# Input first with places of its own for the first weights, and a token-major end, in a fused decoder step

## The chip, the core and the metric

The kernel runs on one core of one Trainium2 chip. The metric is the device time of one launch, in microseconds; lower is better. One launch does the whole step: the two layers, both groups of sequences, and all outputs.

## The reference, cut to what matters

A two-layer decoder trunk for a prompt group (256 tokens, one sequence) and a sample group (8 sequences of 8 tokens), 320 tokens in all, D = 1024. Each layer computes a modulation from a conditioning vector c, a mixer, and a channel mixer; layer 0 has a dense SwiGLU, layer 1 a mixture of 8 experts of which each token uses 2.

```python
mod = (silu(c) @ w_ada[l] + b_ada[l])[:, None, :]
sh1, sc1, g1, sh2, sc2, g2 = jnp.split(mod, 6, axis=-1)
h = _rmsnorm(x, norm_pre_mix[l]) * (1.0 + sc1) + sh1
mix, s_new, v_rows = _mixer(h, ...)                 # first product: h @ w_in
x = x + g1 * _rmsnorm(mix, norm_post_mix[l])
h = _rmsnorm(x, norm_pre_ffn[l]) * (1.0 + sc2) + sh2
f = _swiglu(h, ...) if l % 2 == 0 else _moe(h, ...)
x = x + g2 * _rmsnorm(f, norm_post_ffn[l])          # l = 1: the output y
# _moe: out = sum over experts of combine[..., e] * swiglu_e(h), combine = softmax of the top 2
```

All of it is fp32. The large products are made from operands split into a high part (`float32r`, one pass of TensorE) and a low part, with three products: high x high, high x low, low x high.

## The kernel before, in words

All engines run programs of their own, tied by semaphores. In front of the experts, x is kept with the channels on the partitions (X, eight tiles of 128 channels by 320 tokens).

**Weights.** Up to the experts the weights come as 512 KB units in a fixed list (UNITS, line 152). SyncE (SP) issues one DMA a unit (`load_unit`, line 454) into a ring of nine places (RAW, `RAW_UNITS`); unit n waits until unit n - 9 has been used. Units 0 to 7 are the first modulation group (scale of the first norm), 8 to 15 the second (its shift), 16 and up the first columns of w_in with other modulation groups among them. ScalarE (ACT) makes the high part of a unit (`hi_until`, line 1365), VectorE (DVE) the low part (`lo_until`, line 543).

**Start.** ACT issues the DMAs of c and then x (lines 1459 to 1463); POOL those of the constants (with the identity matrix `ident`) and of small vectors. TensorE (lines 2027 to 2069) waits for the constants, does three fillers (`warm`, line 1898: products of ones whose result nobody reads; each is one of 320 columns), turns c, multiplies units 0 and 1, waits for x and turns it in five pieces that DVE copies to X. ACT squares X, TensorE adds the squares over the partitions (`stat`), ACT takes the root, DVE the reciprocal, TensorE spreads it over the partitions (`spread_rstd`). Between these it makes the rows of the two modulation groups (`rows_unit`, line 1914, one call a unit), turns them (`turn`) and DVE adds the bias (`modulation`, line 553). From the fourth unit of group 1 on, one filler stands behind each unit. Then DVE scales x by group 0, adds the shift of group 1, and ACT and DVE make high and low operand (lines 741 to 767 and 1481 to 1490) for the first operand product, line 1939. ACT also takes an exponential for the lower bounds of the recurrence between the two copies of the rows (line 1479).

**Routing.** Behind the last norm the tokens are stored in rows (HMF, then `h_rows` in HBM, line 512), the router picks two experts a token, and for job 0 the rows of the expert's tokens are gathered by POOL (line 1840), turned by TensorE (`fill`, line 2381) and split (`gathered`, `low_fill`). While it waits TensorE does eight fillers (line 2402). The modulation group of the last gate (index 11) is made in the same stretch (`pause_turned(2)`).

**Jobs.** A job is one expert with up to 128 of its tokens: 35 pairs (512 KB twice, or 384 KB twice) of weights through a ring of seven places (MRAW); ACT makes the high part of each (`m_hi_part`), DVE the low one (`m_lo_part`), up to five pairs ahead. Eight jobs always run, as a loop; up to four extra jobs, for experts with more tokens than 128, run if needed (one does with these inputs), from a second loop whose body is skipped otherwise. At a job's last pair ACT and DVE make the result in rows of tokens (YEH, YEL), and convert the last two of the next job's first pairs. Its tokens are added to the sums SA (channels on the partitions) in the next job, by products with a placement matrix PTS (`combine`, line 2394). So that the last job can convert "next" pairs too, SP loads five pairs that nobody multiplies (line 526).

**End.** Behind the last job (line 2504 and down; DVE lines 1335 to 1355; ACT lines 1720 to 1727): the last job's tokens are added to SA tile by tile (TensorE, then DVE, then ACT's square); DVE multiplies by the gate (AM); sum of squares, root, reciprocal, spread; DVE scales SA and adds it to X; TensorE, behind 13 fillers, turns X to rows of tokens; ACT and DVE copy them; SP writes them out. POOL has always 13 gathers in its program, one behind another; those that no job has used are released by a marker that DVE sets when the last job is done (line 1337).

## Time and profile before

| | us |
|---|---|
| median of 3 runs | 2127.05 |
| lowest and highest | 2126.18 to 2130.05 |
| the profiled execution's own time | 2128.88 |
| its span, first to last instruction | 2127.0 |
| TensorE products busy in it | 2058.9 (97%) |
| VectorE busy | 1449.0 (68%) |
| ScalarE busy | 1140.9 (54%) |
| mean granted clock of TensorE | 0.987 |

The profile is of one execution. Its span is what the trace covers; 1.9 us of the execution's time lie outside. PE is the row of TensorE's products and PEld that of its weight loads, which run beside them. `<-` behind an idle time names what ended it; "issue" is time in which the engine waited for nothing that the profile shows. PEclk is the granted clock, 1.00 for 2.4 GHz and 0.50 for 1.2 GHz.

### The profile page before, as it was taken

Reading aid. Unit: us, or ns where it says so; the run is one execution under the profiler, and the core shown is the slowest. Engines: PE = TensorE matmul, PEld = TensorE weight load, DVE = VectorE, ACT = ScalarE, POOL = GpSimd, SP = SyncE. Lnnn points to the kernel's source line nnn. Section 1 sums busy time; section 2 is a strip of 40 time slices with the busy share of each in tenths; the row PEclk is TensorE's granted clock in tenths of the full one; section 3 lists DMA queues with packets and bytes.
Section 4 is the critical chain, followed back from the end, with each engine's and each line's share of the span. In section 5 each row is a group of like instructions: output and inputs, shape, how many; then the busy total and the mean of one; then the engine's idle time right before and its main releaser. Section 6 shows DMA issues by size and latency. Waiting matters only on the chain. (4 is left out here: it accounts for less than half of the span.)

```text
span 2127.0 us, 34921 instructions
## 1 busy us (share of the span) xinstructions
PE 2058.9 (97%) x13483; PEld 1843.5 (87%) x13483; DVE 1449.0 (68%) x1610; ACT 1140.9 (54%) x1149; POOL 131.9 (6%) x170
## 2 busy tenths in 40 slices
PE   7999999999999999999999899999999999999997
PEld 4999999888999899989999688888888888888885
DVE  4476545555444456745454689898989898898986
ACT  3434334344333343432443568686777777686764
POOL 2200003200000030000230100000000000000000
PEclk9999999999999999999999899999999999999998
DMA  9635465564666454435654599999999999999994
GB/s 314 214 109 164 129 197 172 194 192 132 216 198 222 125 180 128 125 106 171 188 171 159 201 329 393 327 398 334 372 361 353 374 327 400 327 400 330 391 343 179
DMA packets 244643, 528.79 MB, mean 249 GB/s; under 512 B 18199, under 2 KB 142217, under 8 KB 244530
## 3 DMA queue, kind: packets, MB, share of 16 engines
q1 hardware_dynamic: 234512, 496.56, 66.5%
q0 software_dynamic: 9648, 29.29, 4.4%
q8 instruction: 81, 1.33, 0.3%
q10 hardware_dynamic: 370, 1.35, 0.2%
q14 instruction: 32, 0.26, 0.0%
HBM read 514.54 MB, written 12.59 MB: 248 GB/s over the span
## 5 line engine op out<-in xcount | busy, mean ns | idle before, releaser
L1665 ACT ACTIVATE mhi<-mraw 128x2048 fp32r<-128x2048 f32 (+1 forms) x320 | 579.3, 1821 | 216.1 <-DMA mraw<-in_w_exp_up 89.7
L1135 DVE TENSOR_TENSOR mlo<-mraw,mhi 128x2048 fp32r<-128x2048 f32 (+1 forms) x319 | 681.2, 2164 | 10.3 <-ACT mhi L1665 9.7
L549 DVE TENSOR_TENSOR wlo<-raw,whi 128x1024 fp32r<-128x1024 f32 x244 | 289.1, 1212 | 313.6 <-ACT whi L1373 312.7
L1939 PE MATMUL ps<-h1h,whi 128*128 128x320 f32 x1248 | 386.1, 322 | 7.2 <-DVE h1l L656 3.9
L1940 PE MATMUL ps<-h1l,whi 128*128 128x320 f32 x1248 | 371.6, 310 | 0.0
L2426 PE MATMUL ps<-mhi,xeh 128*128 128x512 f32 (+1 forms) x864 | 327.4, 379 | 2.1 <-DVE xel L1154 1.7
L2427 PE MATMUL ps<-mhi,xel 128*128 128x512 f32 (+1 forms) x864 | 322.0, 373 | 0.0
L1373 ACT ACTIVATE whi<-raw 128x1024 fp32r<-128x1024 f32 x244 | 247.8, 1046 | 119.2 <-PE ps L2325 44.8
L1939 PEld LDWEIGHTS ps<-h1h,whi 128*128 128x128 f32 x1248 | 236.2, 189 | 23.7 <-issue 18.0
L1940 PEld LDWEIGHTS ps<-h1l,whi 128*128 128x128 f32 x1248 | 236.3, 189 | 0.0
L2432 PE MATMUL ps<-mlo,xeh 128*128 128x512 f32 (+1 forms) x864 | 225.0, 372 | 0.0
L1985 PE MATMUL ps<-h1h,wlo 128*128 128x320 f32 x1248 | 209.3, 310 | 0.0
L1985 PEld LDWEIGHTS ps<-h1h,wlo 128*128 128x128 f32 x1248 | 189.0, 188 | 0.4 <-issue 0.4
L2426 PEld LDWEIGHTS ps<-mhi,xeh 128*128 128x128 f32 x864 | 162.7, 188 | 23.3 <-issue 2.0
L2427 PEld LDWEIGHTS ps<-mhi,xel 128*128 128x128 f32 x864 | 162.9, 189 | 19.8
L2432 PEld LDWEIGHTS ps<-mlo,xeh 128*128 128x128 f32 x864 | 159.7, 188 | 22.9
L2463 PE MATMUL ps<-mhi,gth 128*128 128x512 f32 x396 | 157.8, 399 | 0.0
L2464 PE MATMUL ps<-mhi,gtl 128*128 128x512 f32 x396 | 154.7, 391 | 0.0
L2469 PE MATMUL ps<-mlo,gth 128*128 128x512 f32 x396 | 106.3, 390 | 0.1
L2469 PEld LDWEIGHTS ps<-mlo,gth 128*128 128x128 f32 x396 | 74.3, 188 | 16.3 <-DVE mlo L1135 0.5
L2464 PEld LDWEIGHTS ps<-mhi,gtl 128*128 128x128 f32 x396 | 74.5, 188 | 14.3
L2463 PEld LDWEIGHTS ps<-mhi,gth 128*128 128x128 f32 x396 | 74.4, 188 | 14.4
(394 smaller groups left out, 2686.9 us busy)
## 6 DMA issues: line engine op xcount, KB each, us to landing
mraw<-in_w_exp_down SPq DMA_DIRECT2D x198, 512.0 KB, 8.3
mraw<-in_w_exp_gate SPq DMA_DIRECT2D x154, 512.0 KB, 5.3
mraw<-in_w_exp_up SPq DMA_DIRECT2D x144, 512.0 KB, 6.5
raw<-in_w_in SPq DMA_DIRECT2D x128, 512.0 KB, 3.9
raw<-in_w_ada SPq DMA_DIRECT2D x72, 512.0 KB, 3.7
mraw<-in_w_exp_gate SPq DMA_DIRECT2D x72, 384.0 KB, 3.6
mraw<-in_w_exp_up SPq DMA_DIRECT2D x72, 384.0 KB, 4.6
pause<-in_w_ada SPq DMA_DIRECT2D x24, 512.0 KB, 6.5
```

The source lines that it names most:

```text
L549: V.tensor_tensor(WLO[:, u % RAW_UNITS, 0:w], RAW[:, u % RAW_UNITS, 0:w], WHI[:, h % HI_UNITS, 0:w].bitcast(F32), ALU.subtract).then_inc(l ...
L1135: V.tensor_tensor(MLO[:, n % RAW_RING, 0:w], MRAW[:, n % RAW_RING, 0:w], MHI[:, n % HI_RING, 0:w].bitcast(F32), ALU.subtract).then_inc(m_l ...
L1373: A.activation(WHI[:, h % HI_UNITS, 0:w], RAW[:, u % RAW_UNITS, 0:w], ACT.Copy).then_inc(hi_made, 1)
L1665: A.activation(MHI[:, n % HI_RING, 0:w], MRAW[:, n % RAW_RING, 0:w], ACT.Copy).then_inc(m_hi, 1)
L1939: M.matmul(out_, w, v[0], start=start, stop=False, skip_group_check=True)
L1940: M.matmul(out_, w, v[1], start=False, stop=False, skip_group_check=True)
L1985: ins = M.matmul(PS[:, 2 * j + m, 0:T], w[1][:, s], parts[0][:, k * T:(k + 1) * T], start=False, stop=(k == KD - 1), skip_group_check=True)
L2426: M.matmul(o_, XEH[:, k, :], hi_[:, s], start=(k == 0), stop=False)
L2427: M.matmul(o_, XEL[:, k, :], hi_[:, s], start=False, stop=False)
L2432: ins = M.matmul(PS[:, GROUP_BANKS[g][2 * i + j], 0:w], XEH[:, k, :], lo_[:, s], start=False, stop=(k == KD - 1))
L2463: M.matmul(PS[:, DOWN_BANKS[h], :], GTH[:, kf, :], hi_[:, s], start=(kf == 0), stop=False)
L2464: M.matmul(PS[:, DOWN_BANKS[h], :], GTL[:, kf, :], hi_[:, s], start=False, stop=False)
```

## The change

**Start.** x is loaded by SP, in front of all weights, no longer by ACT. Units 0 to 7 get places of their own (in memory that the operands take later), each with a semaphore of its own; the ring of nine places begins with unit 8, so the first unit that waits for a place is unit 17. TensorE's first three fillers become six products of 128 columns of ones that don't wait for the constants; units 0 and 1 are multiplied behind the turning of x; the five fillers among the rows of group 1 go, and three stay behind its turning instead of four. ACT loads the root's table before it squares (a small root of ones), and the exponential for the lower bounds comes behind the operand pieces.

**Routing.** The gate of the last step is computed here (`gate_dve(1, 48, G2)`), and TensorE makes from it GT: the gate in token-major form, 128 partitions by 1024 channels for the prompt (all rows alike) and 64 by 1024 for the samples. That takes 16 fp32 products with the identity and four copies by ACT. It sits between the pick and the gathered rows, with three fillers behind it instead of eight. DVE first waits until the stored rows are in HBM, since the new tables lie where they came from.

**Jobs.** The conversions of pairs 3 and 4 (ACT) and 2 and 3 (DVE) of a job are made at its head instead of at the end of the job before. Three pairs that nobody multiplies are loaded instead of five.

**End.** TensorE turns the old sums SA straight into the accumulators (six tiles: three groups of tokens by two halves of the channels; `is_transpose`), and adds the last job's tokens with two products of 512 columns a tile. ACT squares each tile with a sum along it (`accum_out`), DVE multiplies it by GT; the root and reciprocal of a [128, 3] table follow. TensorE turns X into banks that have come free, and DVE adds the scaled tile to it. SP writes each 128 tokens as they are ready.

```diff
+GT_BANKS = ((2, 3), (5, 1))
+Z_BANKS = ((0, 1), (4, 5), (6, 7))
+XT_BANKS = ((2, 3), (0, 1), (4, 5))
+LAST_TILES = [(t, h) for t in range(3) for h in range(2)]
+        def raw_count(u):
+            return 16 * (u // RAW_UNITS + (u % RAW_UNITS >= KD))
# SP
-                if n >= RAW_UNITS:
+                if n < KD:
+                    sp.dma_start(PAUSE[1][n][:, :].unsqueeze(1), src).then_inc(first_in[n], 16)
+                    return
+                if n >= KD + RAW_UNITS:
                     sp.wait_ge(unit_used, n - RAW_UNITS + 1)
+            sp.dma_start(XTM[:, 0:2, :], a["x_prompt"][0].rearrange("(t p) d -> p t d", p=P)).then_inc(xtm, 16)
+            sp.dma_start(XTM[0:TS, 2, :], a["x_sample"].rearrange("s t d -> (s t) d")).then_inc(xtm, 16)
             for n in range(len(UNITS)):
...
-            for n in range(HI_RING):
+            for n in range(HI_RING - 2):
...
+            for t in range(2):
+                sp.wait_ge(sem("y_out"), 2 * t + 2)
+                sp.dma_start(out["yp"][0, P * t:P * t + P, :], XTM[:, t, :]).then_inc(sem("y_stored"), 16)
# DVE, routing
+            pause_turned(2)
+            gate_dve(1, 48, G2)
+            dve.wait_ge(hd_stored, 16 * TT)
+            V.tensor_copy(GE[:, :, :].rearrange("p k (s t) -> p k s t", s=NS), seq(AM)).then_inc(sem("ge_made"), 1)
             m_lo_part(0, 0)
             m_lo_part(0, 1)
-            pause_turned(2)
...
             def job_dve(job, first=False):
+                m_lo_part(job, 2)
+                m_lo_part(job, 3)
                 for p in range(PAIRS):
...
-                        m_lo_part(job, p + HI_RING - 2)
-                    if p != PAIRS - 2:
+                    if p < PAIRS - 2:
                         m_lo_part(job, p + HI_RING - 1)
# DVE, end
+            see.step(V.memset(ZS[:, :, :], 0.0), sem("zs_zero"))
+            dve.wait_ge(sem("gt_out"), 4)
+            for i, (t, h) in enumerate(LAST_TILES):
+                n, g = (P, 0) if t < 2 else (TS, 1)
+                dve.wait_ge(sem("z_squared"), i + 1)
+                V.tensor_tensor(XTM[0:n, t, 512 * h:512 * h + 512], PS[0:n, Z_BANKS[t][h], :],
+                                GT[0:n, g, 512 * h:512 * h + 512], ALU.mult).then_inc(sem("z_gated"), 1)
+            see.step(V.tensor_tensor(ZT[:, :], ZS[:, 0, :], ZS[:, 1, :], ALU.add), sem("z_summed"))
+            see.next(sem("z_root"))
+            st(V.reciprocal(ZT[:, :], ZT[:, :]))
+            for t, h in LAST_TILES:
+                see.next(sem("xt_in"))
+                V.scalar_tensor_tensor(XTM[0:n, t, 512 * h:512 * h + 512], XTM[0:n, t, 512 * h:512 * h + 512],
+                                       ZT[0:n, t:t + 1], PS[0:n, XT_BANKS[t][h], :], ALU.mult, ALU.add)\
+                    .then_inc(sem("y_out"), 1)
# ACT, start, routing and end
+            A.activation(ROOT1[:, :], ONES[:, 0:1], ACT.Sqrt)
             act.wait_ge(aux_out, 6)
...
+            act.wait_ge(hd_stored, 16 * TT)
+            act.wait_ge(sem("gt_in"), 1)
+            for g in range(2):
+                for h in range(2):
+                    n = (P, TS)[g]
+                    A.activation(GT[0:n, g, 512 * h:512 * h + 512], PS[0:n, GT_BANKS[g][h], :], ACT.Copy)\
+                        .then_inc(sem("gt_out"), 1)
             for k in range(2):
                 gathered(k, k)
...
+            A.activation(ROOT1[:, :], ONES[:, 0:1], ACT.Sqrt)
+            see.next(sem("zs_zero"))
+            for i, (t, h) in enumerate(LAST_TILES):
+                n = P if t < 2 else TS
+                act.wait_ge(sem("z_in"), i + 1)
+                A.activation(ZQ[0:n, i, :], PS[0:n, Z_BANKS[t][h], :], ACT.Square, accum_out=ZS[0:n, h, t:t + 1])\
+                    .then_inc(sem("z_squared"), 1)
+            see.next(sem("z_summed"))
+            A.activation(ZT[:, :], ZT[:, :], ACT.Sqrt, bias=EPST[:, 0:1], scale=1.0 / D).then_inc(sem("z_root"), 1)
# TensorE, routing and end
-            warm(8, 3)
+            pe.wait_ge(sem("gate_made"), 4)
+            pe.wait_ge(sem("ge_made"), 1)
+            pe.wait_ge(sem("hm0_out"), TT)
+            for g in range(2):
+                for d in range(KD):
+                    gate = GE[:, d, :] if g else AM[:, d, 0:1].broadcast_to([P, P])
+                    ins = M.matmul(PS[0:(P, TS)[g], GT_BANKS[g][d // 4], d % 4 * P:(d % 4 + 1) * P], gate, ident,
+                                   start=True, stop=True, skip_group_check=True)
+            ins.then_inc(sem("gt_in"), 1)
+            warm(3, 4)
...
-            warm(4, 7)
+            pe.wait_ge(m_aux_out, extra * JAUX + (NE * JAUX + AHEAD))
+            for t, h in LAST_TILES:
+                for d in range(4):
+                    M.matmul(PS[0:n, Z_BANKS[t][h], d * P:(d + 1) * P], SA[:, 4 * h + d, t0:t0 + n], ident,
+                             start=(d == 0), stop=False, is_transpose=True, skip_group_check=True)
             pe.wait_ge(y_made, extra + (NE + 1))
+            for t, h in LAST_TILES:
+                M.matmul(PS[0:n, Z_BANKS[t][h], :], PTS[:, t0:t0 + n], YEH[:, s], start=False, stop=False,
+                         skip_group_check=True)
+                M.matmul(PS[0:n, Z_BANKS[t][h], :], PTS[:, t0:t0 + n], YEL[:, s], start=False, stop=True,
+                         skip_group_check=True).then_inc(sem("z_in"), 1)
+            for i, (t, h) in enumerate(LAST_TILES):
+                if t:
+                    pe.wait_ge(sem("z_gated"), i - 1)
+                for d in range(4):
+                    ins = M.transpose(PS[0:n, XT_BANKS[t][h], d * P:(d + 1) * P], X[:, 4 * h + d, t0:t0 + n], ident)
+                ins.then_inc(sem("xt_in"), 1)
```

## Rows read from the trace of the kernel before

**Rows 1.** By stage: window, length; busy PE, PEld, DVE, ACT, POOL; clock, DMA share, GB/s.

```profile
0.00:41.30 41.30, 28.71 (x262) 14.80 (x262) 11.72 (x32) 11.47 (x21) 5.56 (x19) 0.96 0.88 308
41.30:52.10 10.80, 7.75 (x48) 6.97 (x48) 8.84 (x22) 6.52 (x13) 5.45 (x9) 1.00 0.96 334
52.10:1211.50 1159.40, 1121.13 (x8755) 1050.19 (x8753) 618.31 (x898) 466.74 (x627) 108.28 (x131) 0.99 0.54 168
1211.50:2089.60 878.10, 877.53 (x4276) 754.66 (x4277) 789.02 (x626) 644.70 (x474) 9.82 (x9) 1.00 0.96 358
2089.60:2127.00 37.40, 23.74 (x147) 16.91 (x145) 21.10 (x35) 11.49 (x17) 2.83 (x3) 0.76 0.25 83
```

**Rows 2.** Chain that ended last, behind the last job: start, length (us), what.

```profile
2092.82 0.08 DVEq L1332
...
2095.29 0.80 issue
```

**Rows 3.** By stage again, the start cut finer for the DMA.

```profile
0.00:15.00 15.00, 5.66 (x26) 3.21 (x30) 0.45 (x3) 2.34 (x2) 4.99 (x18) 1.00 0.88 291
15.00:25.00 10.00, 8.43 (x122) 4.92 (x114) 4.02 (x9) 3.71 (x9) 0.00 (x0) 1.00 1.02 397
25.00:30.00 5.00, 3.35 (x28) 1.99 (x32) 0.65 (x1) 0.89 (x2) 0.00 (x0) 0.73 0.36 145
```

**Rows 4.** Order of time, the start: start, length, engine, line, operation, count, wait.

```profile
9.01 3.57 PE L1901 MATMUL ps<-cf,ones 128*128 128x320 f32 x6 [9.01 <-DMA cf<-in_const_f]
...
15.89 1.64 PE L2045 MATMUL ps<-cf,xtm 128*128 128x128 f32 x8
...
20.78 2.99 ACT L1393 ACTIVATE t<-x 128x320 f32<-128x320 f32 x8 [14.64 <-DVE x L730]
...
24.28 1.28 ACT L1405 ACT_TABLE_LOAD   x1 [0.52 <-PE ps L1868]
...
28.01 3.22 PE L1910 MATMUL ps<-raw,csf 128*9 128x256 f32 x32
...
33.86 3.22 DVE L751 SCALAR_TENSOR_TENSOR ht<-x,am,ps 128x256 f32<-128x256 f32 x8
...
37.64 0.62 PE L1910 MATMUL ps<-raw,csf 128*9 128x256 f32 x8
```

**Rows 5.** Busy time in a stretch of the start.

```profile
28.00:30.00 2.00, 2.00 (x21) 0.77 (x24) 0.00 (x0) 0.00 (x0) 0.00 (x0) 0.50 0.03 12
```

**Rows 6.** Order of time, the routing and the start of job 0.

```profile
1203.37 2.25 POOL L1840 DMA_INDIRECT xg<-h_rows,idx  x1 [21.31 <-DVE idx L1149]
...
1209.51 1.08 ACT L1670 ACTIVATE xeh<-ps 128x512 fp32r<-128x512 f32 x2 [6.04 <-PE ps L2385]
...
1211.56 0.67 PE L2426 MATMUL ps<-mhi,xeh 128*128 128x512 f32 x1 [1.65 <-DVE xel L1154]
```

**Rows 7.** Groups by line: one fp32 product of 128 columns is two records.

```profile
L2235 PE MATMUL ps<-im,ktm 128*128 128x128 f32 x256 | 33.4, 274 | 0.0
```

**Rows 8.** Order of time, the head of an expert job.

```profile
1411.14 6.68 DVE L1135 TENSOR_TENSOR mlo<-mraw,mhi 128x2048 fp32r<-128x2048 f32 x3
...
1416.14 1.07 PE L2432 MATMUL ps<-mlo,xeh 128*128 128x512 f32 x4
```

**Rows 9.** Order of time, the end.

```profile
2089.64 1.26 ACT L1698 ACTIVATE yeh<-ps,sw 128x512 fp32r<-128x512 f32 x2 [0.87 <-PE ps L2469]
2090.36 1.41 DVE L1288 SCALAR_TENSOR_TENSOR yel<-ps,sw,yeh 128x512 fp32r<-128x512 f32 x2 [1.10 <-ACT yeh L1698]
...
2101.64 0.95 POOL L1840 DMA_INDIRECT xg<-h_rows,idx  x1 [3.71 <-DMA xg<-h_rows,idx]
...
2108.41 9.40 PE L1901 MATMUL ps<-cf,ones 128*128 128x320 f32 x26
...
2117.65 2.78 PE L2518 MATMUL ps<-cf,x 128*128 128x128 f32 x24
...
2119.59 1.88 DVE L1355 COPY xtm<-ps 128x512 f32<-128x512 f32 x3 [4.98 <-PE ps L2518]
```

More of the change, by code:

```diff
@@ L398, in build @@
         raw_in = [sem(f"raw_in{n}") for n in range(RAW_UNITS)]
+        first_in = [sem(f"first_in{n}") for n in range(KD)]
         hi_made, lo_made = sem("hi_made"), sem("lo_made")
@@ L1477, in _ @@
             rows_copy(0)
-            see.next(sem("lb_shifted"))
-            A.activation(LT[:, 0:2, :], LT[:, 0:2, :], ACT.Exp).then_inc(sem("lb_exp"), 1)
             rows_copy(1)
@@ L1490, in _ @@
                                  bias=MOD[:, mod_tile(0, SH1) + d, 0:1]).then_inc(sem("h_hi"), 1)
+            see.next(sem("lb_shifted"))
+            A.activation(LT[:, 0:2, :], LT[:, 0:2, :], ACT.Exp).then_inc(sem("lb_exp"), 1)
             hi_until(HI_UNITS)
@@ L2054, in _ @@
             M.transpose(PS[:, b, P:P + 82], VR[0:82, 1, :], CF[0:82, C_ID:C_ID + 82]).then_inc(aux_in, 1)
-            for k in range(2, 5):
+            for k in range(2):
                 rows_unit(k, k, 2)
@@ L2058, in _ @@
                 stat(k == 0, k == KD - 1)
+            rows_unit(2, 2, 2)
+            rows_unit(3, 3, 2)
             spread_rstd(4)
-            for k in range(5, KD):
+            for k in range(4, KD):
                 rows_unit(k, k, 2)
```

82 lines of the change are left out of this document (26 added, 56 removed).

## Prediction

> **What bounds the kernel now.** I read the busy time by stage first [rows 1]. TensorE is busy 877.5 of the 878.1 us of the nine expert jobs (eight, and one of the extra ones) and 1121 of the 1159 us of the layers ahead of them: these stages run at TensorE's pace, and a change that only shifts them shifts the end by as much. Two stretches are not at its pace: the first 41.3 us, where TensorE has 28.7 us of work, fillers among them, and the last 37.4 us with 23.7 us, again fillers among them, at a granted clock of 0.76. The change works in both, and a little at the routing. So I read next the chain of waits behind the last job [rows 2], the DMA by stage [rows 3], and the order of time at the start [rows 4], at the routing, at a job's head and at the end.
>
> **The start.** The first product waits for the shift of modulation group 1, whose last weights (unit 15) are multiplied at 37.64 us [rows 4]; the product follows at 41.3, where the second stage of rows 1 begins, 3.7 us later. What holds unit 15 back is a stall: with nine places, units 9 and up wait for units that TensorE uses only after it has turned x, and x lands at 15.89. DMA moves 291 GB/s up to 15 us, 397 up to 25 and then 145 up to 30 [rows 3]. With eight places more, all of units 0 to 16 are issued with no wait. Bytes: x 1.31 MB, constants and conditioning 0.40, sixteen units of 0.524: 10.1 MB. By 25 us 291 x 15 + 397 x 10 = 8.3 MB have moved in any case; the other 1.8 MB take 4.5 us at 397: unit 15 is in at 29.5 us, unit 7 (5.9 MB) at 18.9, unit 16 (first of w_in) at 30.8. The product then comes at 29.5 + 3.7 = 33.2, 8.1 us earlier.
>
> Does the other input arrive in time? x is first in SP's queue: with the constants 1.7 MB, at 291 GB/s 6 us, in by 7. The constants, which TensorE's first product waits for until 9.01, decide, and behind them the turning of c. The turning of x starts near 11 instead of 15.89, at the low clock, and takes 5 us instead of the 4.9 from 15.89 to the squares at 20.78: squares from 16. The squares and their sums take 3.5 us as before (20.78 to 24.28), the root's table load of 1.28 us is out of the chain, and root, reciprocal and spread take 2.45 (from its end at 25.56 to 28.01): 22 us. Then five row products; the row at 28.01 has four of them in 3.22 us at half clock: 4.0, so 26. From there to the end of the scaled x is 5.8 us (31.23 to 37.08) [rows 4]: 32 us, when DVE could have had the shift at 31.2. So this branch, not DMA, ends last by 0.8 us if the clock stays low, and 1.5 us ahead if it is high. I take 7.2 us for the start. Bounds: 9, with the clock high throughout, and 4, if the constants or x land 3 us later than I think and the clock stays low through the first products.
>
> The Exp for the lower bounds is moved behind the operand pieces on ACT: its table load and itself, 1.5 us, come inside the 10.8 us of the first operand products, in which ACT has 6.5 us of work [rows 1]; nothing, at most 0.3.
>
> The five fillers between the row products go, and TensorE then waits for weights, with 0.6 us of work (the row at 37.64) to 0.8 (at 28.01) in the 1.3 us that a unit of 0.524 MB takes at 397 GB/s [rows 3, 4]. In this trace it was at the low of its two levels (1.2 instead of 2.4 GHz) after a pause: the stretch at 28 us has a granted clock of 0.50 [rows 5]. The three fillers left, six records like the six of 3.57 us at 9.01 [rows 4], reach from 31.5 to 35 at that clock: up to 1.8 us behind the operands. The products that follow wait for DVE twice anyway (7.75 us of work in 10.8 [rows 1]), which swallows most of it. The Trainium skill's page "TensorE: Matmul & The Clock Gate" (Part 1, the HAM clock gate) speaks against this edit: the low clock is the default and only recent activity lifts it. The trace agrees; by it the rival "cold start" below gets its chance.
>
> On the table load the Trainium skill ("ScalarE: Activation LUTs", What ACT_TABLE_LOAD costs) counts 1.28 us and as much again for a drain, 2.66 in all. The row has 1.28 us and the root right behind it [rows 4]; by the page's figure ACT's squares at the end would begin 1.4 us later and that branch would end at 2108.4, a fifth of a microsecond behind the sum below. The measured duration decides.
>
> **The routing.** Gate tables are now made here, under the gather. Before, ACT gets the gathered rows, turned, at 1209.51, and job 0 begins at 1211.56 [rows 6]. New work on TensorE: from 1203.9 (DVE's index is out before the gather's start at 1203.37, say at 1202.5, and it has then the modulation, the gate and a copy of 512, by size 0.3 + 0.2 + 0.7 us) 16 fp32 products of 128 columns, two records each of 0.13 us [rows 7]: 4.3 us, then three fillers instead of eight, 1.6: 1209.8. On ACT four copies of 512 (0.54 each, as the two of 1.08 in rows 6) from 1208.3 hold the high halves of the gathered rows until 1210.6, where they began at 1209.51: 1.1 us late, and so is job 0. The wait of DVE for the stored rows costs nothing, as the gather waits for the same. Low side: -0.6, if the clock, low in the first 3 us of job 0 before, stays high. High side: +5.4, if the sixteen products run at half clock. I take +1.1. The two low parts on DVE move from before to after the job's start in the same order: nothing.
>
> **Job boundaries.** Two conversions each on ACT and DVE pass from the end of a job to the head of the next, same order. What changes is that the loop's jump has no conversion queued in front of it. In the chain behind the last job DVE's queue spends 2092.82 to 2095.29, 2.5 us, on the three extra jobs not taken [rows 2], 0.8 a jump at most. The conversion at 1411.14 is the first of three and its product is read at 1416.14 [rows 8]: over 2 us to spare. Nothing.
>
> **The end.** Before: last product to end of span, 37.4 us. After: the high half of the last sums comes as before at 2089.64, DVE's low half ends at 2091.77 [rows 9]. TensorE meanwhile turns the old sums: 24 transposes, 2.8 us as the 24 at 2117.65, to 2092.4; then 12 products of 512 columns at 0.23 [rows 8], the first pair at 2092.9, the last at 2095.2. ACT: its sequencer too has 2.5 us of jumps behind 2090.3, then the root's table load and a small root, 1.5: 2094.3 is the first square, not 2092.9. Six squares of 512 with a sum: 0.63 each from the two at 2089.64 (1.26), 0.7 with the sum, whose cost no row shows (bounds 0.54 and 1.0): 2098.5. DVE's product follows each (0.7): 2099.2; sum, root, reciprocal 0.8: 2100.0; six combined operations of 0.71 (two in 1.41 at 2090.36): 2104.3. The output: before, 5.5 us from the last copy (2121.47) to the end, with 1.31 MB; now only 0.26 MB follow the last operation, at 0.8 for issue, 1.0 and 0.9: 2107.
>
> Beside it runs POOL's chain: the gathers left over, three where one extra job is used, start when DVE sets the marker and are 4.6 us apart (2096.98, 2101.64 and so on, [rows 9]), 14.6 us from marker to last landing. The marker comes at 2093.6 (the second low half is issued when the first ends, near 2091.05, and 2.5 us of jumps follow), so this ends at 2108.2. It was hidden; it now ends last, by about a microsecond. The end: 2127.0 - 2108.2 = 18.8 us gained. What is gone: two conversions on ACT and DVE (4.5 us, 2091.68 to 2096.16), sums handed back and forth one by one with their squares, and 13 fillers of 9.4 us, behind which the last transposes began only at 2117.65. Bounds: 20, if the jumps are cheaper; 14, if squares take 1.0 and TensorE's and ACT's jumps add 2 us more.
>
> **Sum.** -7.2 + 1.1 - 18.8 = -24.9. Against the profiled execution (span 2127.0, its own time 2128.9) this is a span of 2102.1; the median of the runs, 2127.05, lies 1.8 below the profiled one's time, and 2127.05 - 24.9 = 2102. What this kernel's measurement can tell from no change is 0.2%, 4.3 us.
>
> **Rivals.**
> - Cold start (0.13): x and constants later, low clock through the first products, the start gives 3 us or less: 2107. For it: fillers gone, and 0.50 in rows 5; against it: DVE's pace hides much.
> - Gate tables at half clock or ACT's copies worse than thought (0.10): +4.3 at the routing: 2106.5. For it: TensorE now waits for DVE just before, where it had fillers.
> - The end is bound by ACT, squares at 1.0 and longer jumps (0.09): 2106.
> - The uncovered jump (0.03): a jump at a job's end, now in front of DVE's and ACT's next conversions, has 2 us to spare; what it costs over that stops TensorE at each of eight boundaries. From 5.1 us a jump on (8 x 3.1 = 25) the gain is used up; at 5.7 it is 8 x 3.7 = 29.6, a kernel slower than before, 2131.6. Against it: 0.8 us is the longest piece in rows 2.
> - The end hardly gains (0.03): 2120 and more, if the output is held by something that the rows don't show.
>
> The forecast has 0.62, its own range 2097 to 2105.5; the range over the first three rivals is 2097 to 2110. Faster 0.95, same 0.02, slower 0.03.
>
> **What would show it.** Right: DMA near 397 GB/s without a gap from 15 to 30 us; the first operand product near 34; job 0 about 6 us earlier than 1211.56; TensorE still over 99% busy in the jobs; some 19 us from the last expert product to the end, with a gather last. Wrong: a first product behind 38, a gap in front of job 0 of over 4 us more, idle TensorE at a job's head, or an end stretch over 24 us.

## The result, and where the time went

The first comparison gave 2114.1 us against 2128.6 (medians of four runs each), a ratio of 0.9941 with an interval of 0.9922 to 0.9960; a second, with six runs of the changed kernel and sixteen of the one before, gave 2110.9 against 2128.7, ratio 0.9932 (0.9915 to 0.9949). The medians differ by 14.4 and 17.8 us, and both intervals lie below 1. I had forecast a gain of 24.9 us (2102.0), with a range that ended at 2110: the direction was right, the gain 7 to 10.5 us too large.

The stages of the changed kernel's trace, in the columns of [rows 1] (window, length; busy PE, PEld, DVE, ACT, POOL; clock, DMA share, GB/s), and behind them the start cut finer as in [rows 3]:

```profile
0.00:34.30 34.30, 23.26 (x257) 13.81 (x257) 11.95 (x32) 10.23 (x20) 5.55 (x19) 1.00 0.97 355
34.30:45.30 11.00, 7.82 (x48) 7.05 (x49) 8.36 (x20) 6.55 (x14) 5.03 (x8) 1.00 1.07 371
45.30:1204.20 1158.90, 1118.71 (x8776) 1049.82 (x8775) 619.65 (x902) 470.29 (x632) 107.27 (x132) 0.99 0.54 169
1204.20:2085.00 880.80, 877.90 (x4278) 753.05 (x4279) 790.06 (x626) 654.85 (x483) 9.82 (x9) 1.00 0.95 354
2085.00:2107.70 22.70, 8.05 (x60) 6.80 (x58) 9.53 (x18) 6.56 (x17) 2.83 (x3) 0.75 0.39 127
...
0.00:15.00 15.00, 8.79 (x46) 7.49 (x46) 3.59 (x8) 3.83 (x4) 4.98 (x18) 1.00 0.87 308
15.00:25.00 10.00, 9.31 (x164) 4.46 (x162) 2.69 (x10) 3.70 (x10) 0.00 (x0) 1.00 1.02 408
25.00:30.00 5.00, 2.48 (x32) 0.47 (x32) 4.15 (x10) 0.00 (x0) 0.00 (x0) 1.00 1.04 391
```

The start is as forecast: 391 GB/s where 145 stood, and the second stage begins at 34.3 instead of 41.3. The end fell from 37.4 to 22.7 us, not to 18.6. And the stage that I had charged with nothing, the nine jobs, grew from 878.1 to 880.8 us; TensorE is idle 2.9 us in it where it was idle 0.6, and ScalarE has 10 us more of work. The layers' 1158.9 us hide a gain and a loss (the router is reached sooner, the routing is longer). All the pieces, from one trace of each kernel that was run (the experiments below name them):

```
us             first    to the   to the  pick to  nine    end      span   mean
               product  router   pick    job 0    jobs    stretch         clock
before          41.35   1143.6   16.27   10.39    878.1   37.4    2127.0  0.987
after           34.30   1141.2   16.64   12.10    880.8   22.7    2107.7  0.992
after_again     35.22   1138.4   19.18   12.21    881.0   22.5    2108.5  0.989
start_only      35.28   1140.8   18.49   10.39    876.1   37.4    2118.5  0.988
rest_only       40.05   1140.8   14.43   13.32    881.4   22.5    2112.4  0.991
jobs_only       41.91   1144.3   16.43   10.40    882.6   32.2    2127.9  0.987
silu_first      34.29   1142.6   19.26   12.12    877.5   22.5    2108.3  0.989
sums_first      34.16   1145.8   18.15   12.09    876.7   22.5    2109.4  0.987
gathers10       35.40   1144.9   18.57   11.87    881.2   16.7    2108.6  0.987
routing         34.38   1142.1   14.42   11.51    881.1   22.5    2106.1  0.990
combo_dyn       34.59   1139.5   18.19   10.43    877.7   16.6    2097.0  0.992
combo_sums      34.48   1137.3   16.63   10.44    876.4   16.6    2091.9  0.994
combo_nofill    34.97   1144.0   14.43   11.50    875.7   16.6    2097.2  0.988
combo_zs        34.46   1146.2   16.42   10.46    875.7   15.8    2099.1  0.990
```

The columns are: the first operand product; from it to the router's first product; from there to the pick; to job 0's first product; to the high half of the last sums (yeh); to the end. They add up to the span. Two of them, the layers and the way to the pick, spread over 9 and 5 us between these traces, without order by kernel, and by 2.8 and 2.5 us between the two traces of the changed kernel itself; stretches at half clock fall in other places each time. The whole time follows the clock loosely: among the runs of the kernel before that stand beside the experiments the run with the highest mean clock, 0.993, took 2116.7 us and the one with the lowest, 0.981, took 2136.4. The other four columns repeat within about 0.6 us where the code is the same and no half-clock stretch lies in them, and the reading below goes by these. The profiled execution of the changed kernel is the fastest of its first four, with the highest mean clock (0.992 against 0.986 to 0.988); where the others lost their time no trace shows.

**The start** of the changed kernel, in order of time (start, length, engine, line, operation, count, wait):

```profile
9.93 3.95 PE L2078 MATMUL ps<-cf,xtm 128*128 128x128 f32 x16 [0.33 <-DVE csf L742]
...
20.99 1.92 PE L1940 MATMUL ps<-pause,csf 128*9 128x256 f32 x32
...
27.88 0.62 PE L1940 MATMUL ps<-raw,csf 128*9 128x256 f32 x8 [0.66 <-DMA raw<-in_w_ada]
...
30.53 0.62 PE L1940 MATMUL ps<-raw,csf 128*9 128x256 f32 x8 [0.74 <-DMA raw<-in_w_ada]
...
31.92 1.78 PE L1931 MATMUL ps<-cf,ones 128*128 128x320 f32 x6
34.30 0.39 PE L1973 MATMUL ps<-h1h,whi 128*128 128x320 f32 x1 [0.59 <-DVE h1l L786]
```

x is turned from 9.93, before the 11 that I took; the row products run at the high clock (32 records in 1.92 us, 3.22 in [rows 4]); unit 15 is multiplied at 30.53 and the product follows 3.8 us later. The last five rows of group 1 each wait for their DMA and come 1.28 to 1.36 us apart: the start is now at the pace of the DMA. The other branch, the scaled x, ends at 29.2 (VectorE, 3.22 us from 26.00).

**The routing.** The gate tables between the pick and job 0:

```profile
1194.35 3.14 PE L2441 MATMUL ps<-cf,am 128*128 128x128 f32 x16 [1.42 <-DVE am L702]
1197.42 2.44 PE L2441 MATMUL ps<-cf,ge 128*64 128x128 f32 x16
1199.79 1.88 PE L1931 MATMUL ps<-cf,ones 128*128 128x320 f32 x6
...
1199.96 2.04 ACT L1709 ACTIVATE gt<-ps 128x512 f32<-128x512 f32 x4 [5.56 <-PE ps L2441]
1202.15 1.09 ACT L1693 ACTIVATE xeh<-ps 128x512 fp32r<-128x512 f32 x2
...
1204.20 0.49 PE L2469 MATMUL ps<-mhi,xeh 128*128 128x512 f32 x1 [1.66 <-DVE xel L1176]
```

The sixteen products take 5.5 us, not 4.3, for part of them run at half clock (granted clock 0.62 over the first half of them, 0.78 over the second). ScalarE's gathered rows (xeh) come behind its four copies, which end at 1202.0, and behind their own turning, which TensorE begins at 1201.51 when its three fillers are done; xeh starts at 1202.15. It makes 12.1 us from pick to job 0 against 10.39.

**A job's head.** The boundary behind the second of the nine jobs, in order of time on each engine: the changed kernel (ScalarE, then VectorE, then TensorE's weight load), and the same place in start_only, where the conversions are still at the end of the job before.

```profile
1399.69 1.27 ACT L1728 ACTIVATE yeh<-ps,sw 128x512 fp32r<-128x512 f32 x2 [1.70 <-PE ps L2512]
1400.98 1.28 ACT L1688 ACT_TABLE_LOAD   x1
1402.27 3.72 ACT L1688 ACTIVATE mhi<-mraw 128x2048 fp32r<-128x2048 f32 x2
1406.01 1.28 ACT L1717 ACT_TABLE_LOAD   x1
...
1409.35 4.49 DVE L1157 TENSOR_TENSOR mlo<-mraw,mhi 128x2048 fp32r<-128x2048 f32 x2 [0.57 <-ACT mhi L1688]
1413.76 0.48 DVE L1329 TENSOR_TENSOR sa<-sa,ps 128x320 f32<-128x320 f32 x1
...
1414.29 0.19 PEld L2430 LDWEIGHTS ps<-pts,yeh 128*128 128x128 f32 x1 [0.85 <-DVE sa L1329]
```

```profile
1400.59 1.27 ACT L1708 ACTIVATE yeh<-ps,sw 128x512 fp32r<-128x512 f32 x2 [0.63 <-PE ps L2482]
1401.74 3.72 ACT L1675 ACTIVATE mhi<-mraw 128x2048 fp32r<-128x2048 f32 x2
1405.48 1.28 ACT L1697 ACT_TABLE_LOAD   x1
...
1413.70 0.48 DVE L1316 TENSOR_TENSOR sa<-sa,ps 128x320 f32<-128x320 f32 x1
...
1414.38 0.19 PEld L2410 LDWEIGHTS ps<-pts,yeh 128*128 128x128 f32 x1
```

In start_only the first sum (sa) ends 13.6 us behind yeh, and TensorE's third combine product, which needs it, loads its weights at 13.8: 0.2 us to spare. In the changed kernel there are two table loads. One stands in front of the first two conversions, which start 1.43 us later; the other stands behind them, where start_only has its only one, and holds the conversions that follow. VectorE makes the low parts behind ScalarE's high parts, so it loses 0.4 us to the first load and waits 0.57 us for the third high part, behind the second load. The sum stands behind these low parts in VectorE's queue and starts at 14.1 instead of 13.1, and TensorE waits. The waits of weight loads for that sum over the nine jobs (us, times, longest):

```profile
PEld ps L2430 <- DVE sa L1329: 6.2, 8, 0.9
```

The Trainium skill ("ScalarE activation tables: per-element evaluation and per-set limits", Table sets in the compiler and the runtime) says that the back end places table loads per block, the greedy longest run first. A load of its own at the head of the loop's body is in keeping with "per block"; that it takes one set for the two copies and another from the Silu on is not the longest run, since the copies behind the Silu need no load. The rows decide: two loads at job 0's head and at each of the seven boundaries behind it. Only the head of the extra job, which has a loop of its own, shows none; in start_only it has none either.

**The end**, ScalarE, VectorE, SP, POOL, and the time from issue to landing:

```profile
2084.97 1.27 ACT L1728 ACTIVATE yeh<-ps,sw 128x512 fp32r<-128x512 f32 x2 [0.30 <-PE ps L2512]
...
2089.06 0.60 ACT L1754 ACTIVATE zq<-ps 128x512 f32<-128x512 f32 x1 [0.69 <-DVE zs L1363]
2089.56 0.19 ACT L1754 ACTIVATION_READ_ACCUMULATOR zq<-ps 128x1 f32 x1
...
2088.85 0.15 DVE L1361 COPY spare<-sw 128x1 f32<-128x1 f32 x1 [1.75 <-issue]
...
2094.26 4.03 DVE L1377 SCALAR_TENSOR_TENSOR xtm<-xtm,zt,ps 128x512 f32<-128x512 f32 x6
...
2098.32 0.52 SPq L554 DMA_DIRECT2D out_ys<-xtm  x1
...
2089.75 0.94 POOL L1870 DMA_INDIRECT xg<-h_rows,idx  x1 [46.78 <-DVE spare L1361]
2094.36 0.94 POOL L1870 DMA_INDIRECT xg<-h_rows,idx  x1 [3.67 <-DMA xg<-h_rows,idx]
2099.74 0.94 POOL L1870 DMA_INDIRECT xg<-h_rows,idx  x1 [4.43 <-DMA xg<-h_rows,idx]
...
out_yp<-xtm SPq DMA_DIRECT2D x2, 512.0 KB, 4.8
out_ys<-xtm SPq DMA_DIRECT2D x1, 256.0 KB, 4.3
xg<-h_rows,idx POOLq DMA_INDIRECT x3, 5.1
```

VectorE's last operation ends at 2098.3, 13.3 us behind yeh (forecast 14.7), and the last of the output lands at 2098.3 + 4.3 = 2102.6. A gather ends last, as forecast: the third lands 5.3 us after 2099.74, at 2105.0. But the second and third are 5.4 us apart, not 4.6 as the first and second, and the span goes on for 2.7 us behind the last landing.

### The profile page after: what moved, and what is told of

Read it like the earlier page. It is cut to its first block and busy times, and to the rows that moved or that the text cites. A ratio compares the mean times of both kernels' runs of the same rounds, so it can differ in the third digit from the quotient of the medians.

```text
span 2107.7 us, 34719 instructions
## 1 busy us (share of the span) xinstructions
PE 2035.7 (97%) x13413; PEld 1830.5 (87%) x13413; DVE 1439.6 (68%) x1595; ACT 1148.5 (54%) x1162; POOL 130.5 (6%) x170
## 5 line engine op out<-in xcount | busy, mean ns | idle before, releaser
L1157 DVE TENSOR_TENSOR mlo<-mraw,mhi 128x2048 fp32r<-128x2048 f32 (+1 forms) x317 | 677.1, 2163 | 15.7 <-ACT mhi L1688 14.8
L2475 PEld LDWEIGHTS ps<-mlo,xeh 128*128 128x128 f32 x864 | 159.4, 188 | 22.7
L2512 PEld LDWEIGHTS ps<-mlo,gth 128*128 128x128 f32 x396 | 74.3, 188 | 15.8
L2506 PEld LDWEIGHTS ps<-mhi,gth 128*128 128x128 f32 x396 | 74.4, 188 | 14.4
```

Source lines behind the costliest of these rows:

```text
L1157: V.tensor_tensor(MLO[:, n % RAW_RING, 0:w], MRAW[:, n % RAW_RING, 0:w], MHI[:, n % HI_RING, 0:w].bitcast(F32), ALU.subtract).then_inc(m_l ...
L2475: ins = M.matmul(PS[:, GROUP_BANKS[g][2 * i + j], 0:w], XEH[:, k, :], lo_[:, s], start=False, stop=(k == KD - 1))
L2506: M.matmul(PS[:, DOWN_BANKS[h], :], GTH[:, kf, :], hi_[:, s], start=(kf == 0), stop=False)
L2512: ins = M.matmul(PS[:, DOWN_BANKS[h], :], GTH[:, kf, :], lo_[:, s], start=False, stop=(kf == KF - 1))
```

## The experiments

**after_again**, the changed kernel unchanged.

> The changed kernel once more, unchanged. Its first four runs lay between 2109.5 and 2117.3 us (8 us apart), with the profiled one the fastest, while the kernel before lay within 4 us. Theory (clock): the spread comes from stretches of low granted clock that fall in other places from run to run, so the mean clock of a run and its span go together (0.992 with 2107.7, 0.986 with 2112 to 2115.5 so far), and the middle of five more runs is 2112 to 2115. Rival (fixed loss): there is no such tie, and the five runs lie within 2 us of each other. Ratio to the kernel before expected at 0.993 to 0.994.

Six runs of 2110.3 to 2116.0 us, median 2110.9; the two longest, 2116.0 and 2114.2, are those with the lowest mean clock (0.986, 0.987; the others have 0.988 and 0.989). The tie to the clock holds in this set, and the median is 1.1 us under the expected range.

**start_only**, the kernel before with the start of the change alone.

> The kernel before with the start of the change alone (x first on SyncE, places of their own for the first modulation group, no fillers among the rows, the exponential moved). Theory (it acts as the traces of the two kernels show it): first operand product near 34.3 us instead of 41.35, and all of it reaches the end: 7 us under the kernel before, ratio 0.9967. Rival (clock): with fillers gone the clock is low in more or other places of the first layers, and 1 to 4 us of the 7 are given back in most runs: 3 to 6 us, ratio 0.9972 to 0.9986.

Median of eleven runs 2121.0, ratio 0.9966 (0.9952 to 0.9980): 7.2 us. The first product came at 35.3, not 34.3: its trace is at half clock (0.50) from 30 to 36 us, and those of after_again and gathers10 are too. From the first product to the router the eleven traces with the new start have 1137.3 to 1146.2 us, on average 1142.1, and the three with the old one (before, jobs_only, rest_only) 1140.8 to 1144.3, on average 1142.9: nothing shows that clock is given back later, though the spread of 9 us could hide a few microseconds. The interval of the ratio, 4.3 to 10.2 us, also allows the rival's upper end.

**rest_only**, the changed kernel with the start of the one before.

> The changed kernel with the start of the kernel before (ScalarE loads x behind c, no places of their own for units 0 to 7, fillers among the rows). First operand product at 41.3 to 41.4 us, nine jobs 880.8 to 881.3 us, end 22.5 to 22.8 us: 9 to 10 us under the kernel before, 7 over the changed kernel. Rival (the parts are not independent): the jobs or the end stretch differ by over 1 us from the changed kernel's.

One run, 2114.2 us: jobs 881.4 and end 22.5, as in the changed kernel; the parts are independent there. The first product came at 40.05, over a microsecond earlier than in the two other traces with that start (41.35 and 41.91), and pick to job 0 took 13.3 us, since all sixteen products of the gate tables fell in a stretch of low clock (3.75 and 3.05 us for the two halves, granted clock 0.56 over them).

**jobs_only**, the kernel before with the job part alone:

```diff
             def job_act(job):
+                m_hi_part(job, 3)
+                m_hi_part(job, 4)
                 A.activation(SPARE[:, 0:1], ONES[:, 0:1], ACT.Silu)
...
-                        m_hi_part(job, p + HI_RING - 1)
-                    if p != PAIRS - 2:
+                    if p < PAIRS - 2:
```

> The kernel before with the job part of the change alone (two conversions on ScalarE and VectorE passed from a job's end to the next one's head, three spare pairs loaded instead of five). Theory (table load): the extra table load of 1.28 us is there at each of the eight looped jobs' heads, and the nine jobs take 880.5 to 881.3 us instead of 876.1 to 878.1. Rival (the longer jobs come from the new routing, tables or end): they stay at 876 to 878. In the end stretch the part alone takes away the conversions of 4.4 us behind the last product: 37.4 falls to 33 to 34 us.

Jobs 882.6 us and end 32.2 (expected 33 to 34): the end wins 5.2 us and the jobs lose 4.5 by the two traces. The one run took 2129.7 us, against a median of 2126.2 for the kernel before, whose runs go from 2116.7 to 2133.6. The wait is there, in a kernel with the old start, routing and end:

```profile
PEld ps L2395 <- DVE sa L1304: 5.7, 7, 0.9
```

The job time is 1.3 us over the range expected. The head of job 0 lies in a half-clock stretch (0.50 from 1213.1 to 1216.1), as it does in the kernel before, whose line is this:

```profile
1211.60:1215.00 3.40, 3.40 (x8) 2.67 (x9) 3.40 (x2) 3.38 (x3) 0.00 (x0) 0.52 0.00 0
```

Half of such a stretch is lost by TensorE, 1.6 of these 3.4 us (an estimate from the clock of 0.52). It accounts for most of the 2.0 us by which the kernel before, with 878.1, is longer than start_only, with the same jobs and 876.1. So the change's price in the jobs is 880.8 to 881.4 less 876.1, 4.7 to 5.3 us, of which the two profiled executions set side by side show only 2.7.

**silu_first**, one line moved:

```diff
             def job_act(job):
+                A.activation(SPARE[:, 0:1], ONES[:, 0:1], ACT.Silu)
                 m_hi_part(job, 3)
                 m_hi_part(job, 4)
-                A.activation(SPARE[:, 0:1], ONES[:, 0:1], ACT.Silu)
```

> One line moved: at a job's head ScalarE's small Silu of ones comes in front of the two conversions that the change put there, not behind them. Theory (table load): the conversion in front of the Silu needs a table of its own at the head of the loop's body, 1.28 us more on ScalarE in every job, and that is what makes the nine jobs 880.7 us long instead of 878.0. Without it the jobs are back at 878.0 to 878.3, the wait of TensorE for VectorE's sum in the combine step (2.8 us in all) goes, and the time is 2.5 us under the changed kernel's. Rival (uncovered jump): the loop's jump with no conversion queued in front of it is what costs; then the jobs stay at 880.7 and the time stays within 0.5 us.

One table load a job is left, the nine jobs take 877.5 us, and the time is 2110.5 (2105.7 to 2111.8), a ratio of 0.9917 (0.9899 to 0.9935) where the changed kernel has 0.9932. The expected 2.5 us are not seen in the times (0.4 by the medians), whose intervals overlap; the 3.3 to 3.9 us are seen in the job column. The same boundary as above:

```profile
1405.22 1.28 ACT L1715 ACT_TABLE_LOAD   x1
...
1406.62 9.12 ACT L1688 ACTIVATE mhi<-mraw 128x2048 fp32r<-128x2048 f32 x5
...
1417.44 0.48 DVE L1329 TENSOR_TENSOR sa<-sa,ps 128x320 f32<-128x320 f32 x1
```

The load that is left is again in front of the first two conversions, which start 2.69 us behind yeh (1403.93), no earlier than the changed kernel's 2.58. What is gone is the load behind them, and with it VectorE's wait for the third high part: the sum starts 13.5 us behind yeh instead of 14.1. In start_only it was 13.1. So the wait is not gone:

```profile
PEld ps L2430 <- DVE sa L1329: 2.3, 7, 0.6
```

**sums_first**, both table loads left as they are, VectorE's order changed:

```diff
+                    summed = [u for u in SIDE[p] if u[1] == "combine"]
+                    for s, _, k in summed:
+                        dve.wait_ge(m_aux_in, job * JAUX + (s + 1))
+                        V.tensor_tensor(SA[:, k, :], SA[:, k, :], PS[:, 4 + s % 2, 0:T], ALU.add)\
+                            .then_inc(m_aux_out, 1)
                     if p < PAIRS - 2:
                         m_lo_part(job, p + HI_RING - 1)
```

> The changed kernel with one thing in another order on VectorE: in the pairs 2 to 9 of a job, the sum of the last job's tokens (sa) comes in front of the pair's conversion, not behind it; the extra table load stays. Theory (queue behind the conversions): TensorE's third combine product of a job waits for VectorE's first sum, which stands behind the conversions that now start 1.4 us later; with the sum in front of one conversion of 2.28 us it is in time in spite of the table load. The wait of weight loads for sa (6.2 us in 8 times) goes and the nine jobs fall from 880.8-881.4 to 876 to 877 us. Rival (ScalarE's later high parts hold TensorE itself, or the jobs are longer for another reason, code or records): they stay over 880.

The same lines are taken out where they stood, behind the conversion. Both table loads are there and the jobs take 876.7 us; no wait for the sum is left, only this, of a kind that the kernel before has too (0.5 us, once):

```profile
PEld ps L2515 <- DVE mlo L1157: 0.9, 2, 0.7
```

The time from one job's yeh to the next one's, in the traces above, shows how the loss is made up (differences of the starts of yeh in order of time; the last one ends with the extra job):

```
us                      job 0 to 1   next six, each   to the extra job's
before, start_only      98.0         97.22            97.22
changed kernel          97.9         97.91 to 97.94   97.70
silu_first              98.0         97.35 to 97.37   97.68
sums_first              98.0         97.22            97.23
```

At each of the six boundaries the changed kernel loses 0.7 us: 0.57 by the second load (silu_first takes it away) and 0.14 by the moved conversions with one load in front of them. With the sum ahead of a conversion both cost nothing. The last boundary has no table load and still loses 0.48, in silu_first too. There VectorE passes from its first loop to the second, over a jump, a wait and the reading of the number of extra jobs, and no longer has a conversion queued in front of that. The changed kernel:

```profile
1990.02 6.70 DVE L1157 TENSOR_TENSOR mlo<-mraw,mhi 128x2048 fp32r<-128x2048 f32 x3 [0.61 <-issue]
...
2001.63 0.19 PEld L2430 LDWEIGHTS ps<-pts,yeh 128*128 128x128 f32 x1 [0.61 <-DVE sa L1329]
```

That fits the uncovered jump of my rivals, with 0.2 us to spare instead of 2; no run takes it away by itself. With the sum ahead of a conversion (sums_first) it costs nothing either. So the loss in all its parts comes from the sum that stands behind the moved conversions with 0.2 us to spare; the table loads and, once, this jump use that up.

**gathers10**, POOL's program without the three gathers whose rows no job reads:

```diff
-            for job in range(NE + EXTRA + 1):
+            for job in range(NE + 2):
...
-            pool.wait_ge(xg_in, 16 * (NE + EXTRA + 1))
+            pool.wait_ge(xg_in, 16 * (NE + 2))
```

> The changed kernel with 10 gathers in POOL's program instead of 13: the three whose rows no job reads (with these inputs, where one extra job is used) are left out. Theory (the left-over gathers end last): the last output write lands about 4.7 us ahead of the end of the span with them, and the writes themselves get a little faster since no gather runs beside them; the end stretch falls from 22.8 to 18 us and the time by 4.5 to 5 us. Rival 1 (something behind the output, common to both): the 2.66 us between the last gather's landing and the end of the span stay as they are behind the output's landing; then the gain is 2 us. Rival 2: the writes of the output hold the end in any case, gain under 1 us.

The end is 16.7 us, 5.9 less, more than any of the theories gave; median 2107.2 against the changed kernel's 2110.9, ratio to the kernel before 0.9904 (0.9887 to 0.9920). The last writes:

```profile
2105.30 0.52 SPq L554 DMA_DIRECT2D out_ys<-xtm  x1
...
out_yp<-xtm SPq DMA_DIRECT2D x2, 512.0 KB, 2.6
out_ys<-xtm SPq DMA_DIRECT2D x1, 256.0 KB, 2.9
```

With no gather beside them the writes land after 2.6 and 2.9 us instead of 4.8 and 4.3, and the span ends 0.4 us behind the landing at 2108.2 (span 2108.6). The 2.7 us behind the last gather are tied to a gather being last: six traces with 13 gathers have 2.6 to 2.7 there, and the five without the left-over ones have 0.4 behind the last write. What happens in them no record shows. The Trainium skill ("DMA: Bandwidth & Descriptors", Queues, rings and completion order) says that each DMA engine takes turns, packet by packet, between the queues it has work for; by that writes and gathers slow each other down, and the landings agree.

**routing**, the gathered rows in front of the copies, no fillers there, the table's second half in other banks:

```diff
-GT_BANKS = ((2, 3), (5, 1))
+GT_BANKS = ((2, 3), (5, 4))
...
             for n in range(3):
                 m_hi_part(0, n)
+            for k in range(2):
+                gathered(k, k)
             act.wait_ge(hd_stored, 16 * TT)
...
-            for k in range(2):
-                gathered(k, k)
...
-            warm(3, 4)
```

> The changed kernel with the routing alone mended as in combo_dyn. Theory (the four copies of the gate table and the three fillers stand in front of the gathered rows): pick to the first product of job 0 falls from 12.2 us (with a low clock there; 12.1 in the first profile of the changed kernel) to 10.4 to 10.7, what it is without the gate tables (10.39). Rival (TensorE's 16 products themselves are what is late, 5.6 us at the low clock from 1195.1): they end at the same place, the rows are turned behind them, and only the copies' 2 us less 0.1 or nothing is won: 11.5 and more.

TensorE's wait for the four copies, in front of job 0, goes as well; VectorE waits for them instead, in front of its clearing of SW. One run, 2107.9 us. Pick to job 0 took 11.5 us, as the rival has it. Here all sixteen products ran at a low clock (0.57 granted over them), 3.75 and 2.90 us, as they did in combo_nofill, which has the same routing and also shows 11.5; in the three other kernels below that have it they took 5.5 us together and it is 10.4. Both have a part: copies and fillers in front of the rows cost 1.7 us (12.1 to 10.4), the products a further 1.1 when the clock is low for all of them.

**combo_dyn**, three mends at once; POOL's gathers for extra jobs under a condition each:

```diff
+            for k in range(EXTRA):
+                with pool.If(extra > k):
+                    pool.wait_ge(idx_made, NE + 2 + k)
+                    pool.indirect_dma_start(XG[:, :], None, HD, bass.IndirectOffsetOnAxis(IDX[:, 0:1], 0)).then_inc(xg_in, 16)
+                    pool.wait_ge(xg_in, 16 * (NE + 2 + k))
```

> The changed kernel with three mends: the small Silu in front of the two conversions at a job's head (as in silu_first); POOL issues a gather behind the ninth only for extra jobs that are used, under a condition for each (general, unlike gathers10); and at the routing ScalarE takes the gathered rows in front of the four copies of the gate table, TensorE's three fillers there go, and the sample half of the table lies in banks 5 and 4, which job 0 needs only behind its first sum. By the parts: jobs -3.3 (877.5 instead of 880.9 us), end -5.9 (16.7 instead of 22.6), routing -1.5 (pick to job 0 10.7 instead of 12.2 us): 10.7 us under the changed kernel's 2111 to 2113, so 2100 to 2102, ratio to the kernel before 0.987. Rival: the parts overlap or the conditions on POOL cost as much as a gather saves; 2104 or more.

Median 2099.8 against 2126.2 for the kernel before, ratio 0.9888 (0.9868 to 0.9909). Jobs 877.7, end 16.6, pick to job 0 10.4: each within 0.3 us of what was expected, and the conditions on POOL cost nothing that shows.

**combo_sums**, combo_dyn with VectorE's order of sums_first.

> combo_dyn and sums_first together: the 2.3 us of waits for sa that were left in combo_dyn go, nine jobs 876.1 to 876.6 instead of 877.7 us, end stretch 16.6, and the time is 1.3 us under combo_dyn's (2099.8 against a kernel before of 2126.2): ratio 0.988. Rival: conversions that now start half a microsecond later are late in their turn, jobs 877.5 or more.

Jobs 876.4. The time, 2101.4 in four runs (2093.7 to 2102.9, ratio 0.9884, 0.9868 to 0.9901), isn't under combo_dyn's and can't tell 1.3 us.

**combo_nofill**, combo_sums without the three fillers at the start.

> combo_sums without the three fillers behind the turning of group 1. In four of eight traces with the changed start the first operand product came at 35.2 to 35.4 us with the fillers at half clock in front of it, in the others at 34.3 to 34.6. Theory (fillers only hold the product back): it comes at 34.2 to 34.4, 0 to 1 us earlier, and the first 60 us are no longer otherwise; time 0 to 1 us under combo_sums. Rival (they hold the clock up): the first operand products run at half clock from 34 us on, and what they gain is lost before 60 us: time the same or up to 2 us over.

The product came at 34.97, no earlier (it waited 2.1 us for VectorE's operand), and the clock in 30 to 40 us was 0.52 instead of 0.83 in combo_sums. The time is 2100.0, ratio 0.9877 (0.9861 to 0.9894). Nothing is won or lost that the times can tell. The rival's low clock was there in the one trace, and the stretch before 60 us was not shorter: ScalarE's table load at 47.7 us comes at 47.2 to 47.4 in the other three.

**combo_zs**, combo_sums with the clearing of the table for the sums of squares ahead of the extra jobs' loop.

> combo_sums with VectorE's clearing of the table for the sums of squares moved from behind the extra jobs' loop to in front of it. In the trace of combo_sums ScalarE is ready for the first square at 2078.66 us and waits until 2079.36 for that clearing, which stands behind VectorE's jumps of 1.76 us over the extra jobs not taken. Theory (those jumps now stand in the chain of the output): the first square comes 0.6 to 0.7 us earlier behind the last expert product, the end stretch is 15.9 to 16.1 instead of 16.6 us; in the time this is less than can be measured, 2098.5 to 2101 at a kernel before of 2126 to 2128. Rival (the squares wait for TensorE's tiles): the stretch stays at 16.5 or more.

End 15.8 us, and the first square 3.3 us behind yeh instead of 4.1. The time, 2100.4 (2097.1 to 2101.7), ratio 0.9880 (0.9859 to 0.9901), is the same as that of the three before it within what can be told. These four kernels are 24 to 26 us faster than the kernel before by their ratios, and some 9 to 12 us faster than the changed kernel.

## Why the prediction was wrong, step by step

- The start, -7.2 (bounds 4 to 9): 7.05 in the profiled pair and 7.2 by start_only. The mechanism was right: DMA without a gap, unit 15 last, the table load out of the chain. That the figure fits so well is in part luck: unit 15 was used at 30.5, a microsecond behind the 29.5 of the sum, and the scaled x, taken to end last at 32 with a low clock, ended at 29.2 with a high one. The first product comes at 34.2 to 34.6, or at 35.2 to 35.4 in the three traces at half clock from 30 us on; in combo_nofill, at half clock but without fillers, at 34.97, so of that the fillers have some 0.3 us, not "up to 1.8".
- The rival "cold start" came in part, as that low clock in three of the ten traces with the fillers, at a price of about 1 us for the first product; a gain of "3 us or less" it did not make.
- The routing, +1.1: +1.5 to +1.8 in five traces with the new routing and the new start, +2.9 in rest_only. The mechanism was right; the sixteen products were sized for the high clock, 4.3 us, and take 5.3 to 5.5, and 6.7 in rest_only. The rival "gate tables at half clock" is partly true each time, at 0.4 to 0.7 us over the sum's 1.1 and at 1.8 in rest_only, not at 4.3 (and 2102 + 4.3 is 2106.3, not the 2106.5 that it says).
- **The step that failed is "Job boundaries. ... same order ... Nothing."** It costs 4.7 to 5.3 us. The order on ScalarE is the same, conversions and then the small Silu; but the boundary of the loop's body now lies in front of the conversions, and there they get a table load of their own. And the slack that I read, "over 2 us to spare" [rows 8], was that of the conversion's own reader. The operation queued behind the conversions on VectorE, the first sum, had 0.2 us. With the sum in front of a conversion (sums_first) the jobs are back at 876.7, loads and all. I asked what waits for the moved instruction, not what waits for those behind it.
- I took the 878.1 us of [rows 1] as the jobs' undisturbed length. Up to 2.0 of it was a half-clock stretch at job 0's head; I had named it, at 0.6.
- The end, -18.8 (bounds 14 to 20): -14.7. That POOL's chain ends last was right. It was mis-sized by 4.1 us, the second term that failed. I read gathers 4.6 us apart from a time with no other traffic [rows 9]; beside the output the last two are 5.4 apart and the last one lands after 5.3, so that marker to last landing is 16.2 us and not 14.6. And the 2.7 us from the last landing to the end of the span were put at nothing. The branch I worked out in more detail, ScalarE's and VectorE's, was right within 1.4 us (squares 0.57 apart, not 0.7), and without the gathers that branch ends at 16.7 us. On the root's table the measured 1.28 us held: its root follows right behind, as in [rows 4], with no drain as long again.
- The sum with what was measured: -6.7 for the start (41.35 less 34.7, the mean of the ten first products with the fillers), +1.7, +4.9, -14.7: -14.8, where the runs have -14.4 and, by the second ratio, -14.5. That is closer than the traces warrant: with the mean of the three old first products, 41.1, the start is -6.4, and the two noisy columns are left out.

The range, 2097 to 2110, was built from the rivals' prices; the largest loss was none of them. "The uncovered jump" looked at the right place and came true at one boundary, for 0.5 us, but it was weighed against 2 us of slack where the queue had 0.2.

## What to carry to other kernels

When an instruction is moved, look for the least slack among all that stand behind it in its engine's queue, not for its own reader's; a sum with 0.2 us to spare turned two table loads at a job's head into a loss of 0.7 us a job. Where copies stand at the head of a loop's body and another function behind them, look in the trace for a load in front of each; here the Silu in front of the copies saved one of the two. Work that nobody reads is free only while something else ends last: count the left-over transfers again when the end becomes shorter, with the traffic that will then run beside them.

## What the runs showed of the hardware that I had not expected

- Copies at the head of a loop's body load a table of their own, and the Silu behind them another: 1.28 us each, eight times. The head of the extra job, in a second loop, has neither.
- A square with a sum along it takes a record of 0.60 us and a read of the accumulator of 0.19 to 0.22, and the next one starts 0.56 to 0.59 us after the one before it: the read is nearly hidden.
- Writes of 512 KB to HBM land after 2.6 us alone and 4.3 to 4.8 (medians of six traces) beside gathers; the gathers, of the same size, go from 4.6 us apart to 5.4.
- The span ends 0.4 us behind the last landing when that is a write issued by SP, and 2.6 to 2.7 us behind it when it is a gather issued by POOL.
- The mean clock of runs of one program, on several chips, went from 0.981 to 0.993, and its time from 2136.4 to 2116.7 us; within one set of eleven runs on one chip from 0.982 (2133.6) to 0.993 (2116.7). The profiled execution of the changed kernel (0.992) lies 4.6 us under the median of its set, that of combo_sums (0.994) 7.6 us.
